# A two-block transformer kernel: VectorE splits four parts of the first block's projection weights and sums the twelfth modulation chunk, and normed tiles are turned in four banks

## What is computed

```python
c_act = jax.nn.silu(c)
ada = c_act @ w_ada[layer] + b_ada[layer]            # 1024 x 6144
shift1, scale1, gate1, shift2, scale2, gate2 = jnp.split(ada, 6, axis=-1)
h = modulate(rms_norm(x, norm1_g[layer]), shift1, scale1)   # h * (1 + scale) + shift
proj = h @ w_in[layer]                               # 1024 x 2304
qa, ka, va, qb, kb, vb = jnp.split(proj, IN_SPLITS, axis=-1)
```

## Time and profile before

| what | value |
|---|---|
| runs | 2298.94, 2304.80, 2304.33 us; median 2304.33 |
| the profiled execution | 2306.07 us; its span 2304.3 us |
| PE busy | 2072.7 us (90%), mean granted clock 0.979 |
| DVE busy | 1313.2 us (57%) |
| ACT busy | 879.9 us (38%) |
| POOL busy | 956.1 us (41%) |

### The profile page before, as it was taken

The page is one execution under the profiler, slowest core; times in us unless marked ns, Lnnn a source line. Parts: engine busy times, 40 slices in busy tenths (PEclk is TensorE's granted clock), DMA queues, the critical chain, the costliest instruction groups (busy, mean ns, idle before and its releaser), DMA issues. The chain is left out here.

```text
span 2304.3 us, 21758 instructions
## 1 busy us (share of the span) xinstructions
PE 2072.7 (90%) x6824; PEld 1138.0 (49%) x6824; DVE 1313.2 (57%) x3017; ACT 879.9 (38%) x2292; POOL 956.1 (41%) x625
## 2 busy tenths in 40 slices
PE   7899997888898999888689999999988998999999
PEld 5687542333333333333233333333345555888887
DVE  5133455777778777787464456465546653433432
ACT  2354412444445444445233335344324332321321
POOL 1685004566654665665366775666710100000000
PEclk9999999999999999999899999999998999999999
DMA  8542427999999999999999999999922002222231
GB/s 348 174 146 84 174 110 291 421 417 417 410 410 411 416 422 416 404 421 410 422 415 408 421 422 399 419 420 421 422 99 107 1 1 92 80 103 92 92 109 55
DMA packets 118068, 650.94 MB, mean 282 GB/s; under 512 B 10920, under 2 KB 29376, under 8 KB 46144
## 3 DMA queue, kind: packets, MB, share of 16 engines
q0 software_dynamic: 73728, 536.90, 56.5%
q1 hardware_dynamic: 41280, 107.32, 13.0%
q10 hardware_dynamic: 2944, 5.33, 0.6%
HBM read 647.41 MB, written 2.10 MB: 282 GB/s over the span
## 5 line engine op out<-in xcount | busy, mean ns | idle before, releaser
L912 PE MATMUL bank<-ring,diag 128*128 128x512 f32 x2048 | 992.1, 611 | 159.5 <-ACT diag L1415 157.9
L592 POOL DMA_INDIRECT ring<-in_uv,idx x512 | 802.6, 1568 | 517.6 <-PE bank L912 239.4
L2012 DVE CUSTOM_DVE_ANT_0 zjunk<-ring,h 128x1024 bf16<-128x1024 f32 x512 | 627.2, 1225 | 432.8 <-DMA ring<-in_uv,idx 431.1
L912 PEld LDWEIGHTS bank<-ring,diag 128*128 128x128 f32 x2048 | 367.0, 190 | 719.0 <-ACT diag L1415 438.8
L1409 ACT ACTIVATE zg<-z 128x1 f32<-128x1 f32 x512 | 103.5, 202 | 706.1 <-DVE z L2012 705.6
L1415 ACT ACTIVATE diag<-ident,weight 128x128 f32<-128x128 f32 x512 | 205.5, 401 | 16.8
L536 POOL TENSOR_SCALAR stats<-stats 128x1 f32<-128x1 f32 (+2 forms) x19 | 4.7, 249 | 381.4 <-ACT slot L1513 111.2
L876 PE MATMUL bank<-w_inb,hTb 128*128 128x512 f32 (+1 forms) x320 | 147.1, 560 | 0.0
L2191 DVE TENSOR_TENSOR ml_lo<-mlp_raw,ml_hi 128x2048 fp32r<-128x2048 f32 x32 | 73.4, 2293 | 114.6 <-ACT ml_hi L1544 114.6
L843 PE MATMUL bank<-w_q,h2T 128*128 128x512 f32 x256 | 130.0, 599 | 1.8 <-ACT h2T L1305 1.8
L1544 ACT ACTIVATE ml_hi<-mlp_raw 128x2048 fp32r<-128x2048 f32 x32 | 61.1, 1908 | 121.8 <-PE bank L631 107.6
(11 more groups left out here) (237 smaller groups left out, 2584.7 us busy)
## 6 DMA issues: line engine op xcount, KB each, us to landing
ada_w<-in_w_ada SPq DMA_DIRECT2D x24, 1024.0 KB
mlp_raw<-in_w_up SPq DMA_DIRECT2D x16, 1024.0 KB, 5.4
mlp_raw<-in_w_down SPq DMA_DIRECT2D x16, 1024.0 KB, 5.1
win_raw<-in_w_in SPq DMA_DIRECT2D x9, 1024.0 KB, 7.1
w_inb<-in_w_in SPq DMA_DIRECT2D x8, 1152.0 KB, 26.5
w_q<-in_w_query SPq DMA_DIRECT2D x8, 1024.0 KB, 9.4
ring<-in_uv,idx POOLq DMA_INDIRECT x512
x<-in_x SPq DMA_DIRECT2D x8, 512.0 KB, 12.8
```

What stands on the lines that cost most here:

```text
L592: e.indirect_dma_start(ring[n % RING], None, a["uv"], bass.IndirectOffsetOnAxis(ap=idx[i][:, j:j + 1], axis=0)).then_inc(s[f"d_ring{n % RI ...
L912: t = e.matmul(bank[2 * (i % 2) + half], diag[n % 4], ring[n % RING][:, 1024 + 512 * half:1536 + 512 * half], start=(j == 0), stop=(j == 127))
L2012: e.tensor_tensor_reduce(out=zjunk, in0=ring[n % RING][:, 0:1024], in1=h2[:, i, :], scale=1.0, scalar=0.0, op0=ALU.mult, op1=ALU.add, accu ...
```

## The change

DVE makes the low parts 0 to 3 (new semaphore `v_wlo`), POOL 4 to 8. Chunk 11 moves from PE's eight products to DVE's sum. Tile i is turned into banks 2 and 3 or 4 and 5, so PE waits only for the low halves of two tiles before. DVE's order is norm 0, norm 1, low halves 0, norm 2, norm 3, low halves 1, part 0, low halves 2 and 3, part 1, chunk 11, part 2, copy of item 4, part 3, copy of item 5. PE makes total 8 and 9 ahead of tiles 0 and 1, total 10 ahead of item 0, 11 behind item 0, 12 and 13 behind items 3 and 4 (banks 0 and 1); totals 14 to 23 stand in the loop, most of them one step earlier. ACT splits part 0 behind tile 0, and multiplies chunks 14 and 16 earlier. Chunks 8 and 9 are loaded ahead of `w_in` part 0. POOL's order is chunks 12 to 15, part 4, chunks 16, 17, 18, part 5 and on as before.

```diff
-ADA_PE = (1, 3, 5, 7, 8, 9, 10, 11)
+ADA_PE = (1, 3, 5, 7, 8, 9, 10)
-ADA_STEP = {12: 0, 13: 2, 14: 4, 15: 6, 16: 8, 17: 10, 18: 13, 19: 15, 20: 18, 21: 22, 22: 24, 23: 28}
-MULTIPLY_AT = {u + half: (n, half) for n, u in ((16, 2), (19, 11), (22, 19)) for half in (0, 1)}
+ADA_STEP = {14: 0, 15: 2, 16: 5, 17: 8, 18: 11, 19: 14, 20: 17, 21: 21, 22: 23, 23: 27}
+MULTIPLY_AT = {u + half: (n, half) for n, u in ((16, 1), (19, 10), (22, 18)) for half in (0, 1)}
+def low_done(c):
+    return ("v_wlo", c + 1) if c < 4 else ("g_wlo", c - 3)
...
@@ SP @@
-            load_win(0)
             load_ada(8)
             load_ada(9)
+            load_win(0)
+            load_ada(10)
             load_win(1)
-            load_ada(10)
             load_ada(11)
             load_win(2)
@@ POOL @@
-            win_low(0)
-            win_low(1)
             ada_columns(12)
             ada_columns(13)
-            win_low(2)
             ada_columns(14)
-            win_low(3)
             ada_columns(15)
+            win_low(4)
             ada_columns(16)
-            win_low(4)
             ada_columns(17)
@@ PE @@
-            ada_total(8)
             for i in range(NT):
-                if i < 3:
-                    ada_total(i + 9)
+                if i < 2:
+                    ada_total(i + 8)
                 for g in (0, 1):
                     q.wait_ge(s["v_hn"], 2 * i + 2)
-                    q.wait_ge(s["v_hT"], 2 * i + g - 1)
-                    turn4(bank[2 + g], hn[i % 2], range(4 * g, 4 * g + 4)).then_inc(s["p_hT"], 1)
+                    if i >= 2:
+                        q.wait_ge(s["v_hT"], 2 * i + g - 3)
+                    turn4(bank[2 + 2 * (i % 2) + g], hn[i % 2], range(4 * g, 4 * g + 4)).then_inc(s["p_hT"], 1)
...
+            ada_total(10)
             q.wait_ge(s["v_hT"], 10)
             for n in range(6):
                 if n == 5:
                     scores(0)
                     scores(1)
                 item(n, range(8))
+                if n == 0:
+                    ada_total(11)
+                if n in (3, 4):
+                    ada_total(n + 9)
@@ ACT @@
-            split_win(0)
-            shift_chunk(8)
             for i in range(NT):
-                if i < 3:
-                    shift_chunk(9 + i)
+                if i < 2:
+                    shift_chunk(8 + i)
                 for g in (0, 1):
                     q.wait_ge(s["p_hT"], 2 * i + g + 1)
                     for dst, src in turned(hT[0], i, g):
                         e.activation(dst, src, ACT.Copy).then_inc(s["a_hT"], 1)
+                if i == 0:
+                    split_win(0)
+            shift_chunk(10)
             split_win(1)
             ada_products(12, range(8))
...
-                if n in (0, 4):
-                    ada_products(13 + n // 4, range(8))
+                if n == 0:
+                    shift_chunk(11)
+                if n in (0, 2):
+                    ada_products(13 + n // 2, range(8))
+                if n in (3, 4):
+                    shift_chunk(n + 9)
@@ DVE @@
-            for i in range(NT + 1):
...
+            def win_low(c):
+                q.wait_ge(s["a_whi"], c + 1)
+                if c >= 2:
+                    q.wait_ge(s["p_item"], win_done(c - 2))
+                e.tensor_tensor(win_lo[c % 2], w_raw[c % 3], win_hi[c % 2].bitcast(F32), ALU.subtract).then_inc(s["v_wlo"], 1)
+
+            norm1(0)
+            norm1(1)
+            turned_low(0)
+            norm1(2)
+            norm1(3)
+            turned_low(1)
+            win_low(0)
+            turned_low(2)
+            turned_low(3)
+            win_low(1)
+            ada_columns(11)
+            win_low(2)
...
             copy_item(4)
+            win_low(3)
             copy_item(5)
```

More of the change, by code:

```diff
@@ L28 @@
 a_pq a_pk a_lam a_e2 a_pt2 a_sn a_mx2 a_n3 a_t3 a_ml a_up
-v_const v_c v_ada v_scale v_hn v_hT v_copy v_va v_sink v_s v_pt v_o v_mixA v_mixB v_x1 v_h2 v_best v_ch v_z v_ag v_gain v_hs v_rr v_kn v_rot
+v_const v_c v_ada v_scale v_hn v_hT v_wlo v_copy v_va v_sink v_s v_pt v_o v_mixA v_mixB v_x1 v_h2 v_best v_ch v_z v_ag v_gain v_hs v_rr v_kn v_rot
 v_pq v_pk v_lam v_s2 v_c2 v_pt2 v_o2 v_sn v_mx2 v_x2 v_n3 v_t3 v_ml v_up v_fin
@@ L73, in ada_bank @@
 def ada_bank(n):
-    return n % 2 if n < 12 else 7
+    return n % 2 if n < 14 else 7
 def ada_use(n):
@@ L81, in ada_summed @@
 def ada_summed(n):
-    return 9 * (n // 2 + 1) if n < 8 else sum(4 if m in ADA_ACT else 5 for m in range(12, n + 1))
+    return 9 * (n // 2 + 1) if n < 8 else 45 if n < 12 else sum(4 if m in ADA_ACT else 5 for m in range(12, n + 1))
 def item_chunk(n):
@@ L393, in load_win @@
                 if c >= 3:
-                    q.wait_ge(s["g_wlo"], c - 2)
+                    name, value = low_done(c - 3)
+                    q.wait_ge(s[name], value)
                 e.dma_start(w_raw[c % 3], a["w_in"][c]).then_inc(s[f"d_win{c % 3}"], 16)
@@ L640, in ada_total @@
                 p, total = ada_place(n), bank[ada_bank(n)][:, 0:256]
-                before = n - 2 if n < 12 else n - 1
-                if n == 12:
+                before = n - 2 if n < 14 else n - 1
+                if n == 14:
                     name, value = copied(5)
@@ L656, in ada_total @@
                 else:
-                    q.wait_ge(s["v_ada" if n < 8 else "g_ada"], ada_summed(n))
-                    e.matmul(total, one, ada_sum[n // 2 % 2 if n < 8 else 2 + n % 2], start=True, stop=True).then_inc(s["p_ada"], 1)
+                    q.wait_ge(s["v_ada" if n < 12 else "g_ada"], ada_summed(n))
+                    e.matmul(total, one, ada_sum[n // 2 % 2 if n < 12 else 2 + n % 2], start=True, stop=True).then_inc(s["p_ada"], 1)
             q.wait_ge(s["v_const"], 2)
@@ L691, in item @@
                 b = bank[item_bank(n)]
-                q.wait_ge(s["g_wlo"], c + 1)
+                name, value = low_done(c)
+                q.wait_ge(s[name], value)
                 if n >= 2:
@@ L743, in values @@
                 if t < 2:
-                    q.wait_ge(s["a_shift"], 8)
+                    q.wait_ge(s["a_shift"], 10)
                     q.wait_ge(s["v_scale"], 4)
@@ L1164, in split_win @@
                     q.wait_ge(s["p_item"], win_done(c - 2))
-                    q.wait_ge(s["g_wlo"], c - 1)
+                    name, value = low_done(c - 2)
+                    q.wait_ge(s[name], value)
                 e.activation(win_hi[c % 2], w_raw[c % 3], ACT.Copy).then_inc(s["a_whi"], 1)
@@ L1178, in turned @@
             def turned(h, i, g):
-                part, b = h[:, 4 * g:4 * g + 4, :], bank[2 + g].rearrange("p (k q) -> p k q", k=4)
+                part, b = h[:, 4 * g:4 * g + 4, :], bank[2 + 2 * (i % 2) + g].rearrange("p (k q) -> p k q", k=4)
                 if i == 0:
@@ L1214, in copy_item @@
                 if n < 4:
-                    q.wait_ge(s["p_ada"], 12)
+                    q.wait_ge(s["p_ada"], 11)
                     for dst, src in zip(in_order(qT[:, n, :]), two_parts_in_order(b)):
@@ L1279, in _ @@
                     q.wait_ge(s["p_item"], 22)
-                    q.wait_ge(s["g_wlo"], 9)
+                    q.wait_ge(s["g_wlo"], 5)
                     for half in (0, 1):
@@ L1646, in _, with norm1 @@
                     scale_chunk(n - 1)
-            for i in range(NT + 1):
[L1648 to L1661, removed]
+            def norm1(i):
+                q.wait_ge(s["g_root"], rooted("first"))
+                q.wait_ge(s["v_scale"], 4)
+                q.wait_ge(s[f"d_x{i}"], 16)
+                q.wait_ge(s["p_hT"], 2 * (i - 1))
+                e.scalar_tensor_tensor(hn[i % 2], x[:, i, :], ss1[:, i:i + 1], slot[0], ALU.mult, ALU.mult).then_inc(s["v_hn"], 1)
+                q.wait_ge(s["v_hn"], 2 * i + 1)
+                q.wait_ge(s["a_shift"], 4)
+                e.tensor_tensor(hn[i % 2], hn[i % 2], slot[1], ALU.add).then_inc(s["v_hn"], 1)
@@ new lines, in turned_low @@
+            def turned_low(i):
+                for g in (0, 1):
+                    q.wait_ge(s["a_hT"], turned_hT(i, g))
+                    for (hi, _), (lo, src) in zip(turned(hT[0], i, g), turned(hT[1], i, g)):
+                        e.tensor_tensor(lo, src, hi.bitcast(F32), ALU.subtract).then_inc(s["v_hT"], 1)
+            def win_low(c):
[3 more added lines that the diff above has]
+                e.tensor_tensor(win_lo[c % 2], w_raw[c % 3], win_hi[c % 2].bitcast(F32), ALU.subtract).then_inc(s["v_wlo"], 1)
```

## The result

The changed kernel takes 2296.06 us (median of 6 runs, 2292.68 to 2298.44) where the kernel before takes 2304.0 (6 runs): 7.9 us less, a ratio of 0.9969 with a 95% interval of 0.9956 to 0.9982. The forecast was 17.7 us less, at 2287. The direction is right, the size is less than half of it, and the time lies inside the range of 2279 to 2297 only by a microsecond.

A forecast was written before the change was run, and what follows sets the result against it. The gather is DMA-bound at 413 GB/s, so the change only starts it earlier by cutting PE's waits: 16.9 - 1.0 - 0.7 + 1.5 + 1.0 = 17.7 us off 2304.33 gives 2287 us, range 2279 to 2297.

The forecast's parts named there:

- The price of a total on PE: Total 10 ahead of item 0: 2.2 to 3.7 us with the bias row, done by 51.1 to 52.6 under DVE's cover.
- The new wait at total 11: Between items 0 and 1, PE waits for DVE's sum of chunk 11: 0.4 to 1.9 us, taken as 1.2.
- The first rival: At chunk 11's columns, DVE and GpSimd's first add of chunk 12 block each other: gain only 12.5 to 15.3; chance 0.20.
- the inflated norm: Norm stage: DVE's 5.53 us instruction returns to about 1.3, part of items starting 11.8 us earlier.
- the loads swapped: Before the norm stage: chunk 8 loaded ahead of part 0 lands by 35.7; the 3.44 us load wait is inside the 11.8.
- the fourth part on DVE: Behind the copy of item 4: removes the 6.17 us hole ahead of item 6, plus 1.5 us of clock.
- chunk 16's sum: Attention loop: GpSimd's sum ready at 127.6 while PE comes by at 126.9, 0.7 us lost.
- GpSimd just keeping up: Later totals: GpSimd's 69.2 us of work ends at 196.8, PE wants total 23 at 197.4; the 1.05 us wait goes.
- lead eaten behind 201 us: Third rival, later loads or gather head: loads tied to time rather than events eat the lead, 2304; chance 0.07.
- The 1.0 us charged to ACT's order: Attention loop: ACT's first half of chunk 16 delays the copy of item 7, loss 0 to 1.7 us, taken as 1.0.
- the 17.7 of the sum: Whole kernel: total forecast gain, 16.9 - 1.0 - 0.7 + 1.5 + 1.0 us.
- The slower rival: Totals 16 to 23: delays above 2.2 us each lose the lead, 3.1 us each make it slower, 2311; chance 0.04.

The follow-up runs named there:

- e5: The change with ACT's split 1 ahead of the copy of total 10, and PE's total 10 ahead of the turn of tile 3: 2286.50 us, ratio 0.9924.
- e3: The change, but GpSimd starts chunk 12 only when DVE has the sum of chunk 11: 2293.87 us, ratio 0.9957.
- e2: The change with two neighbours in ACT's queue swapped, split 1 ahead of the copy of total 10: 2286.94 us, ratio 0.9923.
- e4: The kernel before, with low part 3 alone made by DVE behind the copy of item 4: 2297.28 us, ratio 0.9968.
- e1: The change with the modulation sum of chunk 11 given back to PE behind item 0: 2291.07 us, ratio 0.9937.

## Why the prediction was wrong

**The price of a total on PE: the step that failed.** The prediction took the row of 6.54 us with `x16` for a pair of totals, so that one would cost 1.9 to 3.3 us and with the bias row 2.2 to 3.7. It is one total, most of it at half clock. The trace of the kernel before had the next one at full clock:

```profile
45.31 3.72 PE L653 MATMUL bank<-ada_w,late 128*128 128x256 f32 x16
48.96 0.69 PE L655 MATMUL bank<-brow,one 1*128 1x256 f32 x2
```

The code has eight matmuls per chunk, and each float32 matmul stands as two records; the bias row, one instruction, stands as `x2` too, which should have been the warning. A total costs 3.6 + 0.6 = 4.2 us at full clock (e5), and 5.5 in the change (50.52 to 55.99), part of it at half clock behind the 2.53 us for which PE waited ahead of tile 3. Three sentences rested on the price. Totals 8 and 9 were dearer too: tile 1 was to be turned by 42.6 and was by about 45.7, so that DVE, which was never to idle, waited 0.60 us for ACT's copy of tile 0 (40.86) and 1.25 for its fourth norm (45.84), and was done at 54.3 for 53.0. Total 10, begun 1.6 us late for this, was to end by 52.6 "under DVE's cover" and ended at 56.0, with item 0 behind it: of the 3 us by which items came late, DVE's end is 1.3 and total 10 the rest. And through total 10's copy it moved split 1, low part 1 and chunk 11's sum.

**The new wait at total 11: right in kind and place, wrong in size.** It was put at 0.4 to 1.9 us and measured 6.21 (from 61.74, the end of item 0, to 67.95; the sum was forecast for 61.2 and came at 67.80). The chain was named link by link, and each link behind total 10 took what was said (1.91 for the split, 2.29 for the low part). Total 10 ended 3.4 to 4.9 us late, and this went down the chain whole: 67.80 less the port's 2.85 is 64.95, 3.8 behind the forecast. The upper bound of 5.6 that the prediction gave the wait was passed as well, since it held the port but no dearer total.

**The first rival happened, on top.** The prediction gave it 0.20, and 2.4 to 3.7 us for the port plus 1.5 for the clock. It measured 2.85 for the port (e3 against the change) and about 2.6 for the clock: item 1 took some 8 us where full clock gives 5.44. The rival's condition was a sum that ends after GpSimd's first add begins (61.1 forecast, 61.64 measured), and it was the mis-priced total that pushed the sum wholly there. With the sum at 61.0, in e2, it did not happen. So the rival was not independent of the forecast's weakest term, and 0.20 was too low for one whose condition, a sum after 61.1, lay inside the forecast's own 60.4 to 61.9. The clock had a gain too that was not reckoned: with total 10 in the way, item 0 ran at full clock, 5.75 us for 7.0. Up to the end of item 1 the sum against the forecast is thus 3.0 for the late start, less 1.3 for item 0, 5.0 for the wait (6.21 for 1.2), 2.6 for the clock of item 1: 9.3, and the table has 9.0 behind item 4.

**What held.** DVE without the inflated norm; the loads swapped at the price of 0.95 us; the fourth part on DVE worth 7.7 us (8.1 by e4, 8.0 in the table), and covered, though it took 3.06 us beside GpSimd; chunk 16's sum (0.74 for the 0.7 forecast); GpSimd just keeping up, with 0.23 us of waiting at one later total and the 1.05 us gone; nearly no lead eaten behind 201 us. The 1.0 us charged to ACT's order did not come: the wait for the copy of item 7 rose from 0.87 to 1.44, but the next one for a copy of `v` fell from 0.91 to 0.24. In e2, where nothing but the chain is mended, 18.4 us came for the 17.7 of the sum. That agreement should not be read as the sum being right: the dearer totals are in e2 too, with the 3.0 us of late start, and what makes up for them is a cheaper item 0 (1.4), no wait at total 11 (1.2) and a cheaper total 11 (0.5).

**The slower rival** (totals 16 to 23 each 2.2 us late) did not happen: the two waits there were 0.97 us together.

The change as a whole thus brings what its fourth part brings alone. The rest without the twelfth chunk (norm and turn, low parts 0 to 2, loads, later totals) wins 6 us more (e1 against e4), which the twelfth chunk gives back, until ACT's two instructions are swapped. How the 6 us divide among those parts no run shows.

## What to carry to other kernels

Before a count in a merged row becomes a price, match it against the code: one instruction may be two records. When work moves to an engine that can hold it, look at the queue of the engine that feeds it: an instruction that needs nothing stood there behind one that waited for PE, and moving it up one place was worth as much again as the whole change. And after filling or moving a hole on PE, read the clock behind it, since a hole of 2.7 us ahead of the items gave back in clock (e5) what its earlier start had won.

## What the runs showed of the hardware

The chain of small dependent instructions on DVE gave way to single long adds of GpSimd: nine instructions that alone take 4.43 us took 7.28 beside two adds of 2.47 and 1.33 us, and both of those were hardly slower than alone (2.39 and 1.30 in the kernel before). Two of the seven in the middle paid it all: the one begun at 61.95 took 2.44 us and the one at 64.42 took 1.37, for 0.48 each. A single long instruction of DVE was affected both ways: low part 3 took 3.06 us for 2.29 in the change, and 4.20 in e4, and in the change GpSimd's next add took 4.33 for 2.39. DVE's began at 94.25 under a GpSimd instruction that ended at 95.15, and the next of GpSimd's, at 95.23, under DVE's, which ended at 97.31: each waited for the other in turn. This is what the Trainium skill, "SBUF — State Buffer", "Who interferes with whom", states of a DVE instruction with two SBUF inputs beside a GpSimd instruction that reads SBUF. The traces of the kernel before, of the change and of e4 agree with it. The first rival had put the price for the chain at 2.4 us for one add or 3.7 for both; it paid 2.85 beside both, less than the 3.8 us of the adds, in part because the instruction under way when the first add began (61.42) still took its usual time.

The granted clock fell to 0.50, the 1.2 GHz level, for about 17 us in one execution of e3 while PE was busy without a break, with 0.13 us idle from 205 to 217; so there the fall did not follow a hole.
